# Neighbourhood attention in the order of grid columns, each block of 16 columns against 32 columns, with constant masks

## The reference, cut to what matters

```python
rows = t // GRID_W                                        # 8
kh = min(NA_KH, rows)                                     # 8: every row is seen
row_idx = np.clip(r - kh // 2, 0, rows - kh)[:, None] + np.arange(kh)[None, :]
col_start = np.clip(c - NA_KW // 2, 0, GRID_W - NA_KW)    # NA_KW = 16
col_mask = (c[None, :] >= col_start[:, None]) & (c[None, :] < col_start[:, None] + NA_KW)
dr = row_idx - r[:, None] + (NA_KH - 1)
dc = np.clip(c[None, :] - c[:, None], -(NA_KW - 1), NA_KW - 1) + (NA_KW - 1)
bias = rpb[:, dr[:, None, :, None], dc[None, :, None, :]]
q = grid(zq) * NA_DIM ** -0.5
k = grid(zk)[:, row_idx]
v = grid(zv)[:, row_idx]
s = jnp.einsum('brqhd,brkwhd->bhrqkw', q, k).astype(jnp.float32) + bias.astype(jnp.float32)
s = jnp.where(col_mask[:, None, :], s, MASK_NEG)
p = jax.nn.softmax(s.reshape(b, NA_HEADS, rows, GRID_W, kh * GRID_W), axis=-1)
```

## Time and profile before

| | |
|---|---|
| median of 3 runs | 2686.83 us (2684.83 to 2690.34) |
| profiled execution, span | 2688.4 us; its own time is not listed beside it |
| TensorE, matmuls | 2526.6 us busy, 94% of the span |
| TensorE, weight loads | 2049.3 us, 76% |
| VectorE | 1344.7 us, 50% |
| ScalarE | 716.3 us, 27% |
| GpSimd | 1761.7 us, 66% |
| mean granted TensorE clock | 0.969 of full |

### The profile page before, as it was taken

One profiled execution on the slowest core, in us unless ns is written; L12 is line 12 of the kernel. 1 busy time (PEld: TensorE's weight loads), 2 busy tenths in 40 slices (PEclk: granted clock), 3 DMA queues, 4 the chain that ended last, 5 costly groups with the idle time before them and its releaser, 6 DMA issues. The chain is left out here.

```text
span 2688.4 us, 36565 instructions
## 1 busy us (share of the span) xinstructions
PE 2526.6 (94%) x11854; PEld 2049.3 (76%) x11854; DVE 1344.7 (50%) x2632; ACT 716.3 (27%) x1504; POOL 1761.7 (66%) x977
## 2 busy tenths in 40 slices
PE   8898889899999978899998999999999889999998
PEld 6787677688888767688886877777877777787877
DVE  6467887443342575411213566664138434751552
ACT  4205776201101254301112222222016232100001
POOL 4464445587777576577776545455769777687884
PEclk9998889999999989999999999999999999999999
DMA  7681001264653202233332321212423213233332
GB/s 268 190 234 59 1 1 32 94 195 150 195 187 95 62 24 90 70 94 102 94 95 78 97 60 55 62 57 64 109 83 70 82 52 121 81 101 91 90 103 75
DMA packets 420546, 259.73 MB, mean 97 GB/s; under 512 B 62845, under 2 KB 411514, under 8 KB 414018
## 3 DMA queue, kind: packets, MB, share of 16 engines
q1 hardware_dynamic: 395024, 199.47, 25.6%
q10 hardware_dynamic: 25393, 58.63, 6.6%
HBM read 253.86 MB, written 8.10 MB: 97 GB/s over the span
## 5 line engine op out<-in xcount | busy, mean ns | idle before, releaser
L669 POOL TENSOR_TENSOR W<-RAW,zeros 128x1024 fp32r<-128x1024 f32 (+2 forms) x349 | 667.4, 1912 | 656.1 <-PE PA L753 311.1
L676 POOL TENSOR_TENSOR W<-RAW,W 128x1024 fp32r<-128x1024 f32 (+2 forms) x355 | 850.5, 2396 | 50.2 <-PE PA L761 12.7
L750 PE MATMUL PA<-H,W 128*128 128x512 f32 x1288 | 505.0, 392 | 6.4 <-POOL W L669 1.9
L753 PE MATMUL PA<-H,W 128*128 128x512 f32 x1288 | 502.4, 390 | 0.0
L750 PE MATMUL PA<-A,W 128*128 128x512 f32 x944 | 373.5, 396 | 16.5 <-DVE A L2008 10.8
L753 PE MATMUL PA<-A,W 128*128 128x512 f32 x944 | 371.6, 394 | 0.0
L761 PE MATMUL PA<-H,W 128*128 128x512 f32 x1288 | 318.3, 389 | 0.0
L750 PEld LDWEIGHTS PA<-H,W 128*128 128x128 f32 x1288 | 241.9, 188 | 60.9 <-POOL W L669 6.3
L753 PEld LDWEIGHTS PA<-H,W 128*128 128x128 f32 x1288 | 241.8, 188 | 50.2 <-issue 0.5
L761 PEld LDWEIGHTS PA<-H,W 128*128 128x128 f32 x1288 | 241.7, 188 | 50.1
L761 PE MATMUL PA<-A,W 128*128 128x512 f32 x944 | 238.5, 395 | 0.0
(11 more groups left out here) (374 smaller groups left out, 3947.6 us busy)
## 6 DMA issues: line engine op xcount, KB each, us to landing
AD<-in_ada_w_dram ACTq DMA_DIRECT2D x40, 1024.0 KB, 5.1
RAW<-in_w_in_dram SPq DMA_DIRECT2D x160, 256.0 KB, 3.2
RAW<-in_mlp_w_up_dram SPq DMA_DIRECT2D x128, 256.0 KB, 3.1
RAW<-in_mlp_w_down_dram SPq DMA_DIRECT2D x128, 256.0 KB, 3.1
RAW<-in_w_up_dram SPq DMA_DIRECT2D x88, 256.0 KB, 3.1
RAW<-in_nsa_w_in_dram SPq DMA_DIRECT2D x40, 256.0 KB, 4.2
RAW<-in_w_down_dram SPq DMA_DIRECT2D x16, 384.0 KB, 3.4
RAW<-in_swa_w_in_dram SPq DMA_DIRECT2D x20, 256.0 KB, 3.4
```

The costliest lines, as they stand in the source:

```text
L669: e.tensor_tensor(W[0][:, s, 0:kc], RAW[:, s, 0:kc], zeros[:, 0:1].rearrange("p (a b) -> p a b", b=1).broadcast_to([P, kc, P]), ALU.add).t ...
L676: e.tensor_tensor(W[1][:, s, 0:kc], RAW[:, s, 0:kc], W[0][:, s, 0:kc].bitcast(F32), ALU.subtract).then_inc(w_split, 1)
L750: pe.matmul(PA[s][:, 0:n], W[0][:, s, k], hi, start=(k == 0), stop=False)
L753: mm = pe.matmul(PA[s][:, 0:n], W[0][:, s, k], lo, start=False, stop=False)
```

## The change

Queries and keys are put in the order of grid columns (column by column, 8 rows in each). A unit is then a block of 16 columns, in reversed order within the whole, and the keys are laid as inner columns 8 to 55 in three blocks of 16 columns, with the columns 0 to 7 and 56 to 63 as the fourth. A unit meets two of the four blocks, 256 keys, in scores, mask, exponential, scaling and transposes. The products with the values go by key block over the units that see it, 10 a head of 256 or 128 columns in place of 16 of 256. The reordering is done by VectorE where it takes the projections out of PSUM (`query`, `key`, `columns_panel`) and where it adds the two halves of a head (the order is turned back there). The plan is `Plan(2, 2, False, fill=NT)`: a unit has two blocks in the store, the store holds two heads, and the values of a head are read once, after its fourth unit.

The bias comes from a table with 16 shifted copies of the middle 32 columns of each row (made by one transfer at the place of the first old one; the second is gone), one transfer a head of 128 pieces of 1 KB, to a raw tile of 8 x 32. Five additions on VectorE spread it, with a step of 32 elements in the raw tile, over three masks of 256 and add constant masks; those (768 columns) are loaded once before the stage. `consts` loses the old mask.

```diff
...
-    c = np.arange(64)
-    start = np.clip(c - 8, 0, 48)
-    col = np.where((c[None] >= start[:, None]) & (c[None] < start[:, None] + 16), 0.0, NEG)
-    parts["na_cols"] = np.concatenate([col, col], 0)
+    q = np.arange(P)[::-1]
+    edges = [*range(8), *range(56, 64)]
+    for name, b, keys in (("near3", 3, [*range(40, 56)] + edges), ("near12", 1, [*range(8, 40)]), ("near0", 0, [*range(8, 24)] + edges)):
+        col, key = 16 * b + q // 8, np.repeat(keys, 8)
+        first = np.clip(col - 8, 0, 48)
+        parts[name] = np.where((key[None] >= first[:, None]) & (key[None] < first[:, None] + 16), 0.0, NEG)
     off, at = {}, 0
     for n, a in parts.items():
         off[n] = (at, a.shape[1])
...
+            BIAS = sb("BIAS", [P, NEAR_N], F32, one)
+            RPB0 = sb("RPB0", [P, 8, 32], F32, one)
...
-    cst = sb("cst", [P, consts.shape[1]])
+    cst_n = off["near3"][0]
+    cst = sb("cst", [P, cst_n])
     cols = sb("cols", [P, 4, P])
     modT = sb("modT", [P, 2, 48])
     coefA = sb("coefA", [P, 2, 4, DC])
     zeros = sb("zeros", [P, 1])
     rot_r = sb("rot_r", [P, P], F32R)
+    with ExitStack() as over:
+        near = sb("near", [P, NEAR_N], F32, over)
     cosT = sb("cosT", [P, S])
     sinT = sb("sinT", [P, S])
...
     BIASES = [BIAS, BIAS1]
+    RPBS = [RPB0, RPB1]
+    NEAR = [(0, 0, 16, 1), (128, 16, 24, 2), (256, 0, 32, 1), (512, 16, 32, 1), (640, 8, 16, 2)]
...
+    def by_rows(x):
+        return x.rearrange("p (r c) -> p r c", r=8)
+    def by_columns(x):
+        return x.rearrange("p (c r) -> p r c", r=8)
+    def key_columns(dst, src):
+        inner, edges = by_rows(src)[:, :, 8:56], src.rearrange("p (r e c) -> p r e c", r=8, e=8)[:, :, 0:8:7, :]
+        return [(by_columns(dst[:, 0:384]), inner), (dst[:, 384:S].rearrange("p (e c r) -> p r e c", e=2, r=8), edges)]
     def split_q(h, src, lo):
...
-        def __init__(self, blocks, ring, in_h, whole=False):
+        def __init__(self, blocks, ring, in_h, whole=False, fill=None):
...
             self.blocks, self.ring, self.turned, self.halves = blocks, ring, TURNED[in_h], 3 - ring
-            self.score_banks, self.turn_banks, self.fill = (SCORES, TURNS, 0) if in_h else (PS, PT, blocks)
+            self.score_banks, self.turn_banks, self.fill = (SCORES, TURNS, 0) if in_h else (PS, PT, fill or blocks)
...
                 grp.setdefault("all", None)
+                grp.setdefault("turns", [range(0, k, P) for k in grp["keys"]])
...
+    def near_scores(h, keys, u):
+        q = QS[h % 2][:, qcols(u)]
+        blocks = [k[:].rearrange("p (t n) -> p t n", t=NT) for k in keys]
+        return [(q, k[:, 0:NT:3, :] if u == 3 else k[:, 2 - u:NT - u, :]) for k in blocks]
...
     def plan_na():
-        plan = Plan(NT, 1, False)
+        plan = Plan(2, 2, False, fill=NT)
         for h in range(8):
...
             plan.groups.append(dict(
-                need=[("q", h), ("k", h)], need_v=("v", h), head=h, first=True, out=("halves", OF[lo:lo + HD, h // 2, :]), rows=P,
-                keys=[S] * NT, at=[0] * NT, scores=[stacked_scores(h, KK[h % 2], b, 0, S) for b in range(NT)],
-                values=[(VV[h % 2][:, t, :], x, t, a, a + 2) for a in (0, 2) for t in range(NT) for x in range(2)],
-                mask=[BIASES[h % 2][:, 6 - 2 * b:14 - 2 * b, :].rearrange("p a n -> p (a n)") for b in range(NT)], sink=None, gate=None))
+                need=[("q", h), ("k", h)], need_v=("v", h), head=h, first=True, rows=P,
+                out=("halves", by_rows(OF[lo:lo + HD, h // 2, :]), lambda x: by_columns(x[:, ::-1])),
+                keys=[256] * NT, at=[0] * NT, turns=[(P, 0), (0, P), (P, 0), (P, 0)],
+                scores=[near_scores(h, KK[h % 2], u) for u in range(NT)],
+                values=[(VV[h % 2][:, t, :], x, slot, a, z) for t, slot, a, z in (
+                    (0, 1, 2, 4), (2, 1, 0, 2), (1, 0, 1, 3), (3, 0, 3, 4), (3, 0, 0, 1)) for x in range(2)],
+                mask=[BIASES[h % 2][:, a:a + 256] for a in (0, 256, 256, 512)], sink=None, gate=None))
         return plan.number()
...
                         at = int(grp["sink"] is not None)
-                        for a in range(0, grp["keys"][b], P):
-                            mm = pe.transpose(bank[:, a:a + P], w[:, at + a:at + a + P], ident)
+                        for slot, a in enumerate(grp["turns"][b]):
+                            mm = pe.transpose(bank[:, slot * P:slot * P + P], w[:, at + a:at + a + P], ident)
...
         mem_value_take(3)
-        aux(cst[:, split:], T["consts"][:, split:], "masks_loaded")
+        aux(cst[:, split:], T["consts"][:, split:cst_n], "masks_loaded")
...
         out_split(8)
-        aux(T["rpb_rows"][:, 0:8], T["rpb"].rearrange("h (j o) w -> (h j) o w", o=1).broadcast_to([8 * 15, 8, RPB_W]), "rpb_eight")
+        rpb = T["rpb"]
+        aux(rpb_near, bass.AP(rpb.tensor, rpb.offset + 40, [[1, 16], [RPB_W, 8 * 15], [1, 32]]), "rpb_shifted")
...
         out_split(8)
-        act.wait_ge(sem("rpb_eight"), 16)
-        aux(T["rpb_rows"][:, 8:64].rearrange("r (m o) w -> r m (o w)", o=8),
-            T["rpb_rows"][:, 0:8].rearrange("r (m o) w -> r m (o w)", m=1).broadcast_to([8 * 15, 7, 8 * RPB_W]), "rpb_repeated")
...
         def bias_load(h):
-            for r2 in range(2):
-                src = T["rpb_rows"]
-                aux(BIASES[h % 2][r2 * 64:(r2 + 1) * 64],
-                    bass.AP(src.tensor, src.offset + (h * 15 + 1 - r2) * 64 * RPB_W + 63,
-                            [[RPB_W - 1, 64], [64 * RPB_W, NJ], [1, 64]]), f"bias_loaded{h % 2}")
-        act.wait_ge(sem("rpb_repeated"), 16)
+            src = rpb_near
+            aux(RPBS[h % 2][:].rearrange("p a b -> p (a b)"),
+                bass.AP(src.tensor, src.offset + h * 15 * 32, [[8 * 15 * 32, 16], [32, 8], [1, 256]]), f"bias_loaded{h % 2}")
+        act.wait_ge(sem("rpb_shifted"), 16)
         act.wait_ge(panel_ready, HG_OUT_END)
         bias_load(0)
+        aux(near[:], T["consts"][:, cst_n:], "near_loaded")
         bias_load(1)
         phase_end()
...
+        def columns_panel():
+            pa = panel_here()
+            r = c["copied"]
+            if r >= 2:
+                dve.wait_ge(sem("turned"), c["turned"])
+            (inner, a), (edges, z) = key_columns(tmp[r % 2][:], pa[:])
+            dve.tensor_copy(inner, a)
+            dve.tensor_copy(edges, z).then_inc(sem("copied"), 1)
+            c["copied"] += 1
+            dve.wait_ge(sem("copied"), c["copied"])
+            dve.nop().then_inc(panel_free, 1)
         def split_panel(dst, scale):
...
                     now = None
+                elif kind == "query":
+                    pa = panel_here()
+                    dve.tensor_scalar(by_columns(dst[:, ::-1]), by_rows(pa[:]), scale, None, ALU.mult).then_inc(panel_free, 1)
+                    now = None
+                elif kind == "key":
+                    pa = panel_here()
+                    (inner, a), (edges, z) = key_columns(dst, pa[:])
+                    dve.tensor_scalar(inner, a, scale, None, ALU.mult)
+                    dve.tensor_scalar(edges, z, scale, None, ALU.mult).then_inc(panel_free, 1)
+                    now = None
+                elif kind == "value":
+                    columns_panel()
+                    now = lambda dst=dst: take_blocks(dst, N // P)
                 elif kind == "rope":
...
                         dve.wait_ge(sem("lower"), c["lower"])
-                        dve.tensor_tensor(out[1], PO[hd % 2][0:HD, :], tmp[hd % 2][0:HD, :], ALU.add).then_inc(sem("head_out"), 1)
+                        order = out[2] if len(out) > 2 else (lambda x: x)
+                        dve.tensor_tensor(out[1], order(PO[hd % 2][0:HD, :]), order(tmp[hd % 2][0:HD, :]), ALU.add).then_inc(sem("head_out"), 1)
                         c["halves"] += 1
...
             dve.tensor_tensor(Y[:, k, :], pa[:], GATE[:, k, :], ALU.mult).then_inc(panel_free, 1)
-        project([("plain", QN[:, k, :], HD ** -0.5) for k in range(4)] + [("plain", KN[:, k, :], 1.0) for k in range(4)]
-                + [("turn", VN[:, :, k * P:k * P + P], 1.0) for k in range(4)])
+        project([("query", QN[:, k, :], HD ** -0.5) for k in range(4)] + [("key", KN[:, k, :], 1.0) for k in range(4)]
+                + [("value", VN[:, :, k * P:k * P + P], 1.0) for k in range(4)])
         phase_end()
         def mask_bias(i):
             if i % 4 == 0:
                 h = i // 4
                 bias = BIASES[h % 2]
-                dve.wait_ge(sem(f"bias_loaded{h % 2}"), 32 * (h // 2 + 1))
-                link(dve.tensor_tensor(bias[:], bias[:], sl("na_cols").rearrange("p (a n) -> p a n", a=1).broadcast_to([P, NJ, 64]), ALU.add))
+                dve.wait_ge(sem(f"bias_loaded{h % 2}"), 16 * (h // 2 + 1))
+                if h == 0:
+                    dve.wait_ge(sem("near_loaded"), 16)
+                for at, lo, hi, n in NEAR:
+                    end = at + n * (hi - lo) * 8
```

(16 more changed lines are left out.)

## The result

The kernel after takes 2695.62 us (median of 19 runs, 2687.63 to 2701.72), the kernel before 2685.13 us in the same comparison (median of 19, 2681.38 to 2693.35). The ratio of the two is **1.0033, 95% interval 1.0027 to 1.0039**: 9 us slower where 15 us faster was forecast. The profiled execution took 2693.25 us and spans 2691.5 (before 2688.4); its granted clock is 0.966 (0.969).

The account below looks back on a forecast made before the run. It took GpSimd's work to bound the neighbourhood attention; -20.5 + 4.3 + 0.4 + 0.5 = -15.3 us, taken as -15 from a base of 2686.8, gave 2672 us, range 2662 to 2681.

Parts of the forecast that it names:

- The stage lasts as long as GpSimd's work: Neighbourhood attention: GpSimd's scalings and panel splits, 12.0 us a head, set its length; rows fill 88.9 of 90.2 us.
- term (1): GpSimd's 32 scalings of attention weights go from 512 to 256 wide: -20.5 us, all on the path.
- term 9: Transfers of bias table and constants lie beside weight streams ahead of TensorE: 0; at worst one late weight panel, +2 us.
- Term (4): VectorE's work in the attention: 9.2 us a head, staying under GpSimd's 10.1.
- Term (2): Five strided bias adds, 1.9 us a head, hold GpSimd for 0.77 of their length: +4.3 us, from +1.1 to +10.3.
- Terms (3): TensorE's products, transposes and values in the attention: 8.6 us a head, hidden under GpSimd's 10.1.
- (5) to (8): Storage for two heads 0; tail 0; first mask waiting for adds +0.4 us; reordering copies in the projection +0.5 us.
- The two engines hold each other: Rival: each of five bias adds may wait for a GpSimd scaling, 11.5 us a head on VectorE; 2680 us, chance 0.17.
- Slower: Rival: strided adds at 4.9 us a head cost GpSimd all its gain; at 7 us, 2699 us; chance 0.03.
- What would show it: Signs: scalings 0.93 to 1.1 us, adds 0.3 to 0.6, GpSimd near 100% busy mid-stage, last output addition near 2085.

Follow-up runs that it names:

- e3: The kernel before with GpSimd's low split of a weight panel cut to 128 of 1024 elements in this stage; ratio to before 0.9995.
- b3: The kernel after with 12 extra products on TensorE ahead of its wait at each head's start, their result written over; ratio to before 1.0021.
- a4: The kernel after with the five bias adds of a head placed half a head earlier; ratio to before 1.0010.
- c2: a3 with the raw bias read contiguously and the output left in column order (right order of both left out); ratio to before 0.9994.
- c1: The kernel before with the query and key splits of a head one unit earlier; ratio to before 1.0038.
- a3: The kernel after with the query and key splits of a head one unit earlier on ScalarE and VectorE; ratio to before 0.9987.

## Why the prediction was wrong

- **"The stage lasts as long as GpSimd's work."** This step failed. The sum matched the span (88.9 of 90.2 us) because GpSimd's work stretches: its 12.0 us a head held 1.4 us in which it was itself held, and it had fallen behind a loop of the same length. Why the two are equally long isn't shown; the match proved nothing. e3 takes 2 us a head from it and the heads stay. With the bound went term (1), the -20.5 us: the loop contains no scaling at all. What the change does to the loop, from the rows above: key splits 3.43 - 1.77 = +1.66; from there to the next mask 4.15 - 3.57 = +0.58 (dearer output and bias, narrower mask and low part); mask and exponentials 3.81 - 4.73 = -0.92; from the reciprocal to the key splits 1.63 - 1.92 = -0.29. That is +1.0 us a head, against +0.9 measured, and -0.6 without the collision. VectorE's and ScalarE's order of time was read for single durations only; the reciprocal's wait of 1.27 us for ScalarE, shown above, was the sign. This accounts for the stage; the 4 us ahead of it (below, term 9) are a second loss.
- **Term (4), VectorE 9.2 us, with "three splits of query and keys at up to 0.88", hidden.** Mis-sized and not hidden: 1.7 each in the last heads, at the place where TensorE waits. The 0.88 was read under a GpSimd with backlog, which the change removes. The one collision in before, the bias add of 2.35 us, was put aside as "a slow one".
- **Term (2).** The adds are 1.76 us (1.9 taken), so the price at a step was right. Their +4.3 us of holding didn't come: GpSimd rests while they run. They count all the same, since they stand in the loop. The factor 0.77 was also read too low: the pair of 3.37 us is itself held up, an undisturbed one takes 3.11 (2087.91), so an add holds GpSimd for some 1.1 us, all its length.
- **Terms (3) and (5) to (8)** show no miss that counts: products and output (1.12, forecast 1.1) as priced, so also the scalings of term (1); the projection +0.4 (0.5 booked); the first mask 1.68 us behind the first scores instead of 1.33 (+0.35, 0.4 booked); the six products 1.5 us at full clock; the tail behind the last scaling 4.8 us instead of 4.7 (0 booked).
- **Term (9), the transfers, 0.** It looked for a late weight panel in the projection. The first transfer of the constants lands 1.9 us later at the start of the program, and the projection begins some 4 us later on average.
- **The clock.** No term had the half clock after an idle wait. b3 shows that it costs nothing in the order of after; in a4 a mask waits for products at half clock, and what that costs was not tried.
- **The rivals.** "The two engines hold each other" had the mechanism, but at the bias adds, with GpSimd still full, and at 2680 us. It is the low split that holds, at the key splits, and it reaches the other side of zero. "Slower" was given 0.03 for the strides, which c2 finds at half a microsecond a head.
- **What would show it.** Scalings of 0.95 us came; a GpSimd near 100% and a last addition near 2085 did not: 59% and 2104.36.

## What to carry to other kernels

An engine that is busy for all of a stretch need not bound it: follow one unit of work from an operation to the same operation of the next round, over every engine and every program order, and see whether another chain is closed as well. Before relieving GpSimd, list which of VectorE's operations have two SBUF operands and ask at what moment the faster GpSimd will now start its long ones; a backlog had kept them apart. Then move one of the two, or give it to ScalarE, before the shorter work is put in. Where a change widens a table, look also at the transfers that bring other parts of it.

## What the runs showed of the hardware

- A VectorE operation on two SBUF operands that begins while GpSimd's tensor_tensor is under way makes next to no headway until that ends: two key splits 3.43 us beside one of 2.34, and 1.38 alone. The Trainium skill (SBUF — State Buffer, who interferes with whom) says so: the loser blocks and does not share, and the order of issue decides who blocks. The trace agrees on the order too: in c1 the query split (2039.69) came 0.04 us ahead of GpSimd's split (2039.73), took its usual 0.69, and GpSimd's took 2.40 instead of 1.89.
- GpSimd's scalings behave otherwise, though they read SBUF too, and here the measurement departs from that page: they don't block VectorE for their length. A bias add that starts during a scaling lasts 1.09 us, as alone, and the pair of scalings 4.2 us instead of 3.1; in a3 two key splits beside a scaling take 1.56 instead of 1.38 and the scaling 1.37 instead of 0.93. Which property of the instruction makes the difference was not tried.
- VectorE's masks, low parts and additions, which have one operand in PSUM, keep their 0.42, 0.40 to 0.43 and 1.12 to 1.17 us beside either.
